# Expert scores: one 512-column pass for the high and low activation parts, the sum of halves on VectorE, the late products on GpSimd

## The reference, cut to what matters

```python
q = (xt @ w_pq).reshape(n_tok, PEER_HEADS, 2, PEER_HALF)
scores = jnp.einsum('thcd,hckd->thck', q, sub_keys)
s_top, i_top = lax.top_k(scores, PEER_TOPK)             # 16 per half
cand = s_top[:, :, 0, :, None] + s_top[:, :, 1, None, :]
best, pos = lax.top_k(cand, PEER_TOPK)                  # 16 experts per token and head
gate = jax.nn.softmax(best, axis=-1)
...
u = jnp.take(expert_u, idx_b, axis=0)
act = jax.nn.gelu(jnp.einsum('thkd,td->thk', u, xb), approximate=False)
v = jnp.take(expert_v, idx_b, axis=0)
return jnp.einsum('thk,thkd->td', g_b * act, v)
```

## Time and profile before

| | |
|---|---|
| Time, median of 3 runs | 2089.2 us (2087.91 to 2093.54) |
| The profiled execution | 2088.83 us, its span 2087.0 us |
| Granted clock of TensorE, mean | 0.993 |
| Busy share | PE 98%, PEld 88%, DVE 71%, ACT 54%, POOL 26% |
| Chain that ended last | PE 82%, POOL 9%, DVE 3%, issue 3% |

### The profile page before, as it was taken

The page is one execution under the profiler, slowest core; times in us unless marked ns, Lnnn a source line. Parts: engine busy times, 40 slices in busy tenths (PEclk is TensorE's granted clock), DMA queues, the critical chain, the costliest instruction groups (busy, mean ns, idle before and its releaser), DMA issues.

```text
span 2087.0 us, 42378 instructions
## 1 busy us (share of the span) xinstructions
PE 2045.3 (98%) x12326; PEld 1829.7 (88%) x12326; DVE 1487.3 (71%) x2388; ACT 1132.3 (54%) x1955; POOL 550.4 (26%) x385
## 2 busy tenths in 40 slices
PE   8999999979999999999999999999999999999997
PEld 6888888767799999999999999987888888888886
DVE  4555766765588879799999999965555555555557
ACT  4455555444455555466666666554555555555553
POOL 0000330010089999944444444100000000000001
PEclk9999999989999999999999999999999999999999
DMA  7755554656576657555555555557756556655554
GB/s 244 228 172 172 171 169 140 225 160 183 160 198 180 184 162 189 167 168 156 157 159 157 157 159 159 167 194 225 213 194 195 193 191 192 194 194 193 192 191 151
DMA packets 254247, 378.47 MB, mean 181 GB/s; under 512 B 41856, under 2 KB 173056, under 8 KB 253568
## 3 DMA queue, kind: packets, MB, share of 16 engines
q1 hardware_dynamic: 254208, 377.98, 60.2%
HBM read 373.69 MB, written 4.19 MB: 181 GB/s over the span
## 4 chain that ended last, share of the span: by engine, by line
PE 82%; POOL 9%; DVE 3%; issue 3%; DMA 1%; SPq 1%; ACT 1%; POOLq 0%; ACTq 0%; DVEq 0%
PE ps L397 26%; PE ps L399 26%; PE ps L398 26%; POOL split_lo L1651 9%; PE ps L626 3%; PE ps L392 1%; DMA raw<-in_expert_v 1%; DMA raw<-in_w_out 0%; DVE split_lo L1012 0%; SPq L370 0%; DVE x_cols L1221 0%; ACT split_hi L701 0%; DVE end_lo L1506 0%; DVE stats L1516 0%; DMA x_nat<-in_x 0%
## 5 line engine op out<-in xcount | busy, mean ns | idle before, releaser
L1012 DVE TENSOR_TENSOR split_lo<-raw,split_hi 128x512 fp32r<-128x512 f32 x848 | 608.5, 720 | 497.0 <-ACT split_hi L701 495.8
L701 ACT ACTIVATE split_hi<-raw 128x512 fp32r<-128x512 f32 x848 | 534.0, 631 | 568.2 <-PE ps L399 552.2
L397 PE MATMUL ps<-act_hi,split_hi 128*128 128x256 f32 x2048 | 586.0, 286 | 0.8 <-POOL split_lo L1651 0.6
L399 PE MATMUL ps<-act_hi,split_lo 128*128 128x256 f32 x2048 | 579.3, 283 | 0.0
L398 PE MATMUL ps<-act_lo,split_hi 128*128 128x256 f32 x2048 | 579.3, 283 | 0.0
L397 PEld LDWEIGHTS ps<-act_hi,split_hi 128*128 128x128 f32 x2048 | 392.6, 192 | 2.6 <-POOL split_lo L1651 1.9
L398 PEld LDWEIGHTS ps<-act_lo,split_hi 128*128 128x128 f32 x2048 | 392.9, 192 | 0.0
L399 PEld LDWEIGHTS ps<-act_hi,split_lo 128*128 128x128 f32 x2048 | 392.6, 192 | 0.0
L397 PE MATMUL ps<-split_hi,whalf_hi 128*128 128x512 f32 x992 | 386.0, 389 | 1.6 <-DVE split_lo L1012 1.6
L398 PE MATMUL ps<-split_lo,whalf_hi 128*128 128x512 f32 x992 | 385.9, 389 | 0.0
L399 PE MATMUL ps<-split_hi,whalf_lo 128*128 128x512 f32 x992 | 385.9, 389 | 0.0
(11 more groups left out here) (183 smaller groups left out, 2101.0 us busy)
## 6 DMA issues: line engine op xcount, KB each, us to landing
raw<-in_expert_u SPq DMA_DIRECT2D x1024, 128.0 KB, 2.9
raw<-in_expert_v SPq DMA_DIRECT2D x256, 512.0 KB, 3.7
raw<-in_w_in SPq DMA_DIRECT2D x112, 512.0 KB, 3.8
raw<-in_w_out SPq DMA_DIRECT2D x32, 512.0 KB, 4.6
raw<-in_w_pq SPq DMA_DIRECT2D x128, 128.0 KB, 2.8
cst<-in_tables SPq DMA_DIRECT2D x3, 768.0 KB, 5.5
x_nat<-in_x SPq DMA_DIRECT2D x4, 512.0 KB, 7.3
x_dram<-x_cols SPq DMA_DIRECT2D x1, 2048.0 KB, 8.0
```

The lines of the kernel that those rows point to most:

```text
L397: nc.tensor.matmul(acc, l_hi, r_hi, start=first, stop=False)
L399: return nc.tensor.matmul(acc, l_lo, r_hi, start=False, stop=last)
L701: nc.scalar.activation(split_hi[:, q % SPLITS, :], raw[:, q // 2, q % 2, :], ACT.Copy).then_inc(hi_ready, 1)
L1012: vec.tensor_tensor(split_lo[:, q % SPLITS, :], raw[:, q // 2, q % 2, :], split_hi[:, q % SPLITS, :].bitcast(f32), ALU.subtract).then_inc( ...
```

## The change

Five things are changed. (1) `act_hi` and `act_lo` lie side by side in `act_both`, and PE does a block with two matmuls: the high part of the weights by 512 columns, which are the 256 of `act_hi` and the 256 of `act_lo`, into the two halves of the bank, and the low part by the 256 columns of `act_hi`, into the first half. (2) DVE adds the halves of the bank with a `tensor_reduce` over two elements that lie 256 apart (`add_halves`) and writes the sum to SBUF; it sends `score_free`. (3) ACT's GELU works in place on that sum. The GELU of a pair's second tile comes after the split of quarter 6 of the next pair, that of the first tile after the split of quarter 2 of the next pair. (4) `late_tile` is POOL's, between `weigh` and `distances`. (5) The first pass of the ranking loop is written out, since pair 0 has no tile before it.

```diff
+            def two(bank, u_hi, u_lo, k):
+                wide = ps[:, bank, :].rearrange("p (a t) -> p a t", a=2)
+                if k < KT - 1:
+                    nc.tensor.matmul(wide, u_hi, act_both[:, :, k, :], start=k == 0, stop=False)
+                    return nc.tensor.matmul(ps[:, bank, 0:SEQ], u_lo, act_hi[:, k, :], start=False, stop=False)
+                nc.tensor.matmul(ps[:, bank, 0:SEQ], u_lo, act_hi[:, k, :], start=False, stop=False)
+                return nc.tensor.matmul(wide, u_hi, act_both[:, :, k, :], start=False, stop=True)
...
             def gelu(pair, t, is_late):
-                act.wait_ge(split_free, pair * 8 + (Q_U + SPLITS + 4 * t + 4))
+                act.wait_ge(score_free, pair * 2 + (t + 3))
                 if is_late:
-                    act.wait_ge(late_used, pair * 2 + (t + 1 - LATE))
-                    dst = late[:, t, :]
+                    dst = late[:, t % 2, :]
...
-                nc.scalar.activation(dst, ps[:, t, 0:SEQ], ACT.Gelu).then_inc(score_free, 1)
+                nc.scalar.activation(dst, dst, ACT.Gelu).then_inc(gelu_done, 1)
...
                 for q in range(4, 8):
                     split_u(pair, q, part_a)
-                gelu(pair, 0, 0 in late_tiles)
+                    if q == 6 and not (isinstance(pair, int) and pair == 0):
+                        gelu(pair, -1, is_late)
...
                 for q in range(1, 4):
                     split_u(pair + 1, q, next_a)
-                gelu(pair, 1, 1 in late_tiles)
+                    if q == 2:
+                        gelu(pair, 0, is_late)
...
+            def add_halves(pair, t, is_late=False):
+                if is_late:
+                    dve.wait_ge(late_used, pair * 2 + (t + 1 - LATE))
+                    dst = late[:, t % 2, :]
+                else:
+                    dst = wexp[:, bass.ds(pair * 2 + t, 1), :].rearrange("p a t -> p (a t)")
+                dve.wait_ge(split_free, pair * 8 + (Q_U + SPLITS + 4 * t + 4))
+                vec.tensor_reduce(dst, ps[:, t % 2, :].rearrange("p (a t) -> p t a", a=2), AX.X, ALU.add).then_inc(score_free, 1)
+
             def split_turn(pair, k, turns=True):
                 split_u(pair, 2 * k)
+                if k == 2:
+                    add_halves(pair, -1, True)
                 split_u(pair, 2 * k + 1)
+                if k == 3:
+                    add_halves(pair, 0, True)
...
                 turn_u(n + 1, 1, True)
+                if not (isinstance(n, int) and n == 0):
+                    add_halves(n, -1)
...
                 turn_u(n + 1, 3, True)
+                add_halves(n, 0)
...
-                        late_tile(pair, -1)
...
-                        late_tile(pair, 0)
...
+                    def late_tile(pair, t, applied):
+                        pool.wait_ge(gelu_done, pair * 2 + (t + 1))
+                        if applied is not None:
+                            pool.wait_ge(gates_free, applied + 2)
+                        row = wexp[:, bass.ds(pair * 2 + t, 1), :].rearrange("p a t -> p (a t)")
+                        eng.tensor_tensor(row, row, late[:, t % 2, :], ALU.mult).then_inc(late_used, 1)
...
                     with pool.Fori(0, GATES // 2 - 1) as i:
                         for s in range(2):
                             weigh(i * 2 + s, s)
+                            late_tile(i + GATE0, s - 1, i * 2 + s)
                             distances(i * 2 + (s + 2), s, True)
```

More of the change, by code:

```diff
@@ L179, in layer_kernel @@
         score_free = sem("score_free")
+        gelu_done = sem("gelu_done")
         x_in = [sem(f"x_in{i}") for i in range(4)]
@@ L600, in score_pair @@
                     for i in range(4):
-                        last = three(ps[:, q // 4, 0:SEQ], split_hi[:, q % SPLITS, i * P:(i + 1) * P],
-                                     split_lo[:, q % SPLITS, i * P:(i + 1) * P], act_hi[:, q % 4 * 4 + i, :],
-                                     act_lo[:, q % 4 * 4 + i, :], q % 4 == 0 and i == 0, q % 4 == 3 and i == 3)
+                        last = two(q // 4, split_hi[:, q % SPLITS, i * P:(i + 1) * P],
+                                   split_lo[:, q % SPLITS, i * P:(i + 1) * P], q % 4 * 4 + i)
                     last.then_inc(split_free, 1)
@@ L897, in keep_set, with u_pair @@
                                      ACT.Copy).then_inc(set_kept, 1)
-            def u_pair(pair, part_a, next_a, late_tiles=(), groups=None, kept=None, staged_set=None):
+            def u_pair(pair, part_a, next_a, is_late=False, groups=None, kept=None, staged_set=None):
                 for q in range(4, 8):
                     split_u(pair, q, part_a)
-                gelu(pair, 0, 0 in late_tiles)
+                    if q == 6 and not (isinstance(pair, int) and pair == 0):
+                        gelu(pair, -1, is_late)
                 if kept is not None:
@@ L918, in _ @@
             act.wait_ge(x1_out, 16)
-            act.sem_inc(late_used, 2)
             act.sem_inc(set_kept, 2)
@@ L945, in _ @@
                 u_pair(i, True, True)
-            u_pair(PAIRS_A - 1, True, False, (1,))
-            u_pair(PICKS, False, False, (0, 1))
+            u_pair(PAIRS_A - 1, True, False)
+            u_pair(PICKS, False, False, True)
             with act.Fori(GATE0 - 1, GATE0 - 1 + GATES // 2) as i:
-                u_pair(i, False, False, (0, 1), i * 2 - (2 * GATE0 - 2))
+                u_pair(i, False, False, True, i * 2 - (2 * GATE0 - 2))
             with act.Fori(GATE0 - 1 + GATES // 2, PAIRS - 1) as i:
-                u_pair(i, False, False, (0, 1))
+                u_pair(i, False, False, True)
             for q in range(4, 8):
                 split_u(PAIRS - 1, q, False)
+                if q == 6:
+                    gelu(PAIRS - 1, -1, True)
             def split_w(n, t, static=False):
@@ L1299, in _ @@
             TOP_STEPS = 30
+            dve.sem_inc(score_free, 2)
+            dve.sem_inc(late_used, 2)
             dve.wait_ge(turn_done, F_Q + 8)
@@ L1339, in rank_set @@
                 turn_u(n + 1, 3, True)
+                add_halves(n, 0)
                 lc.until(second)
                 vec.max_index(head_p[:, s, 8:16], head_b[:, s, 8:16], rest[:, :]).then_inc(ranked, 1)
-            with dve.Fori(0, PH) as i:
+            lc = LoopChain(0, c0, TOP_STEPS)
+            for s in range(2):
+                rank_set(lc, s, s)
+            assert lc.n == TOP_STEPS, lc.n
+            with dve.Fori(1, PH) as i:
                 lc = LoopChain(i, c0, TOP_STEPS)
@@ L1346, in _ @@
                     rank_set(lc, i * 2 + s, s)
-                assert lc.n == TOP_STEPS, lc.n
             chain.n += PH * TOP_STEPS
[L1350 to L1354, removed]
             def apply_gates(n, parity):
@@ L1398, in _ @@
                 turn_u(SOFT + 1, k, True)
+                if k == 1:
+                    add_halves(SOFT, -1)
+            add_halves(SOFT, 0)
             softmax_start()
@@ L1428, in _ @@
                 turn_u(pair, 1, True)
+                add_halves(pair - 1, -1)
                 lc.until(selected[1])
@@ L1432, in _ @@
                 turn_u(pair, 3, True)
+                add_halves(pair - 1, 0)
                 lc.until(collected[1])
@@ L1448, in _ @@
             softmax_end()
+            add_halves(PAIRS_A - 1, -1)
             dve.wait_ge(lo_ready, Q_U + 8 * PAIRS_A)
+            add_halves(PAIRS_A - 1, 0)
             for k in range(2):
@@ L1483, in _ @@
                 split(Q_V, q)
-            late_tile(PAIRS - 1, 0)
+            add_halves(PAIRS - 1, 1, True)
             split(Q_V, 3)
-            late_tile(PAIRS - 1, 1)
             with dve.Fori(0, HELD_AT // 2 - 1) as i:
@@ L1666, in _ @@
                     eng.memset(wexp[:, kept_rows:NT, :], 1.0).then_inc(ones_ready, 1)
+                    pool.wait_ge(ones_ready, 2)
+                    late_tile(PICKS, -1, None)
                     pool.wait_ge(picks_ready, 1)
@@ L1685, in _ @@
                     distances(0, 0, False)
+                    late_tile(PICKS, 0, None)
                     distances(1, 1, False)
+                    late_tile(PICKS + 1, -1, None)
+                    late_tile(PICKS + 1, 0, None)
                     with pool.Fori(0, GATES // 2 - 1) as i:
@@ L1689, in _ @@
                             weigh(i * 2 + s, s)
+                            late_tile(i + GATE0, s - 1, i * 2 + s)
                             distances(i * 2 + (s + 2), s, True)
-                    weigh(GATES - 2, 0)
-                    weigh(GATES - 1, 1)
+                    for s in range(2):
+                        weigh(GATES - 2 + s, s)
+                        late_tile(GATE0 + GATES // 2 - 1, s - 1, GATES - 2 + s)
+                    with pool.Fori(GATE0 + GATES // 2, PAIRS) as i:
+                        for s in range(2):
+                            late_tile(i, s - 1, GATES)
+                    late_tile(PAIRS - 1, 1, GATES)
                 if n == RSTDS:
```

12 lines of the change are left out of this document (2 added, 10 removed).

## The result

The changed kernel takes 2148.08 us (2142.1 to 2150.09), the kernel before beside it 2090.09. The ratio is 1.0269, with a 95% interval of 1.0252 to 1.0286: 2.7% slower. The forecast was 2111, with a range up to 2136. It was slower, as forecast, and the new wait in the gate pairs is there, but two terms of the sum were far off: the gate pairs, and the index loop, which was put at nothing.

The account below looks back on a forecast made before the run. PE was taken to bound ranking and gate pairs, POOL the index loop. Terms -7.7 + 0 - 0.9 + 32 - 1.3 = +22 on the median 2089.2 gave 2111 us, range 2096 to 2136.

Parts of the forecast that it names:

- What bounds the kernel: Score stage: PE sets the ranking and gate pairs (11.52 and 13.29 us), POOL the index loop (11.94 us).
- The change on PE, 0.43 us per pair: Matmul blocks: 0.3467 us instead of 0.360, 0.0133 less, 32 per pair; 27 us over 64 pairs if PE-bound throughout.
- The change on DVE, 0.64 per addition: Each `add_halves` takes 0.64 us (0.6 to 1.2), two per pair; DVE stays under PE or at it.
- The rival of the slow addition: Each addition takes 1.2 us, lengthening ranking, index loop and gate pairs: +76, so 2165 us; chance 0.07.
- The new wait, 14.3 us per gate pair, +32: Gate pairs: PE waits 0.6 us before each gate step; 14.3 instead of 13.29 us per pair, 32 pairs.
- the chain of 7.04 us: Gate step to next: PE, ACT's split, GELU, late product, distances, weigh sum to 7.04 us against PE's own 6.44.
- The step through `add_halves`: Gate step after quarter 1: GELU needs the addition, ready 3.0 us after the step against ACT's 2.97; adds at most 0.1.
- Index loop, 0 (up to +4), and ranking, -7.7: Index loop POOL-bound before and after, so 0, up to +4; ranking and first pairs gain 18 x 0.43 us.
- the two pairs before the gates: The two pairs between index loop and gates: -0.9 us.
- Late products on POOL: Gate pairs: each late product takes 0.74 us on POOL, as work nothing, but POOL runs in order.
- PE as the bound: PE-bound all the way: gate pairs gain 0.43 us like the others, -24, so 2065 us; faster has chance 0.07.
- The third rival: Gate pairs: the chain as said, but each step nearer 7.5 us, 15.0 per pair; +45, so 2134; chance 0.16.

Follow-up runs that it names:

- the wide matmul alone: Kernel before with only the 512-column matmul added; GELU still from the bank's first half, no addition, so the result lacks a product: 2073.37 us, ratio 0.9936.
- distances first: Changed kernel with one swap in GpSimd's gate loop: weigh, distances, late product instead of weigh, late product, distances: 2085.31 us, ratio 0.9987.
- distances first, first pass written out: On top of distances first, the index loop's first pass is written out, with the addition of halves ahead of the compares there: 2082.69 us, ratio 0.9964.
- the kernel with the old pass there: Distances first, but pairs 0 to 25 keep three 256-column matmuls and GELU from PSUM; the additions begin at pair 26: 2076.63 us, ratio 0.9936.

## Why the prediction was wrong, point by point

**What bounds the kernel:** right for the gate pairs and the index loop.

**The change on PE, 0.43 us per pair:** too much. In the kernel with the wide matmul alone it measured 0.25 in the ranking and 0.31 in the gate pairs, since a block costs 0.350 to 0.352, not 0.3467. I had given this as a bound ("if 512 columns behind 256 cost a bit more"). Why the alternation costs 0.004 to 0.005 more stays open.

**The change on DVE, 0.64 per addition:** right. In the changed kernel it lasts 0.652 into `wexp` and 0.677 into `late` (medians), although its two elements lie 1024 bytes apart. The longest of them takes 0.692. The rival of the slow addition is out.

**The new wait, 14.3 us per gate pair, +32:** the mechanism is shown, by taking distances out of the chain (12.96), by shortening one of its two steps (13.94, forecast 13.9) and by lengthening both. The size was 14.85, +48.0. This is the first failed step, 16 us too low: the chain of 7.04 us measured 7.43. By its parts: from the gate products to ScalarE's split 2.59 (1057.75 - 1055.16) instead of 2.47, as TensorE takes 0.92 us from the gate products to the next block behind its wait (1055.16 to 1056.08), not 0.81; GELU 0.41 instead of 0.38; hand-over to GpSimd 0.27 instead of 0.05. The last is the biggest. I had taken it from a hand-over between ScalarE and VectorE with one wait, and it has two waits with register values here, of which the order is worth 0.08. The step through `add_halves` was not the late one.

**Index loop, 0 (up to +4), and ranking, -7.7:** the second failed step, as large. Together with the two pairs before the gates it was -8.6 and measured +7.7. The starts of ScalarE's splits, eight per pair, give the time of each part (us):

| | pairs 0 to 16 | pair 17 | pairs 18 to 25 |
|---|---|---|---|
| before | 193.9 | 11.5 | 95.0 |
| changed | 190.9 | 18.5 | 99.9 |
| distances first | 190.8 | 18.5 | 99.4 |
| distances first, first pass written out | 190.9 | 12.6 | 103.9 |
| changed, first GELU one split earlier | 194.3 | 17.6 | 95.0 |

So the ranking pairs gained about 0.2 each, pair 17 lost 7.0 and the eight pairs of the loop 4.9. The term of the loop was put at 0 because GpSimd sets the pair's time before and VectorE's work with the additions comes to 11.96 us, no more. VectorE's work did not exceed that. Busy time over six passes of its loop, in the kernel before and then in the changed one:

```profile
789.21:857.34 68.13, 67.50 (x551) 66.20 (x550) 62.57 (x62) 34.50 (x60) 67.41 (x46) 1.00 0.78 189
```
```profile
793.09:870.23 77.14, 72.53 (x396) 62.01 (x396) 70.84 (x74) 37.46 (x64) 69.62 (x50) 0.97 0.60 164
```

A pass holds 70.84 / 6 = 11.81 us of VectorE's work but takes 12.86, and no engine is busy all the time any more, GpSimd neither. Before, a pass took 11.36: VectorE ran through the first ones in 10.6 to 11.1, three of them without an idle moment, and only the last ones took the 11.94 of the row I had read. So it came into the loop late and used its slack to catch up. The additions take that slack, while its idle time stays (5.6 us in six passes before, 6.3 after). VectorE's timeline in the kernel before and then in the changed one shows where it comes from:

```profile
856.17 1.25 DVE L1270 STREAM_TRANSPOSE u_cols<-raw 128x1024 f32<-128x1024 f32 x1 [1.26 <-POOL split_lo L1651]
857.34 2.36 DVE L1410 TENSOR_TENSOR onehot<-pos_f,small 128x512 f32<-128x512 f32 x2
```
```profile
855.89 1.25 DVE L1280 STREAM_TRANSPOSE u_cols<-raw 128x1024 f32<-128x1024 f32 x1 [0.89 <-POOL split_lo L1674]
857.06 0.65 DVE L1292 TENSOR_REDUCE wexp<-ps 128x512 f32 x1
857.63 3.19 DVE L1431 TENSOR_TENSOR onehot<-pos_f,small 128x512 f32<-128x512 f32 x2
```

The addition stands behind a transpose that waits for GpSimd. The compares behind it take 3.19 us in this pass instead of 2.36, but over six passes 15.9 instead of 15.1, so their length is the smaller part. The addition returns a bank and releases a GELU, and the waits go round. Waits of the changed kernel between 760 and 910 us (us in total, times, longest):

```profile
ACT wexp L878 <- DVE wexp L1292: 16.0, 7, 6.5
POOL split_lo L1674 <- ACT split_hi L869: 14.5, 13, 5.8
PE ps L598 <- DVE wexp L1292: 11.5, 5, 5.7
DVE u_cols L1280 <- POOL split_lo L1674: 10.5, 13, 1.6
```

ScalarE's GELUs and TensorE wait for the additions, GpSimd for ScalarE, and VectorE for GpSimd. That ring of waits was not in my list. The longest wait is that of pair 17, for the addition behind the softmax's start and the index loop's first operations:

```profile
789.00 0.79 PE L598 MATMUL ps<-act_both,split_hi 128*128 128x512 f32 x1 [5.71 <-DVE wexp L1292]
```

The granted clock from 786 to 797 us is 0.69 behind that wait. That the loss in pairs 0 to 25 comes from the additions and what hangs on them is shown by the kernel with the old pass there (330.2 us) and by the wide matmul without additions (903.9 - 577.3 = 326.7 us to the first gate step). The table's last row shows that the loss of pairs 18 to 25 is not the additions' work as such: every addition is there, only a GELU stands one split earlier, and the pairs take 95.0 us again, while the ranking gets slower by 3.4. Why the GELU's place does both, and which wait of the ring carries the loss, was not tested.

**Late products on POOL:** 0.74 as on the line; the work is hidden, the order isn't. The 0.61 on VectorE in the earlier trace rows holds a stretch of 0.33 us beside GpSimd's `weigh` (1065.38 to 1065.71); where GpSimd has nothing to do, behind the gate steps, the same product takes 0.40 in the kernel before.

**The rivals:** PE as the bound was met in the gate pairs with distances first, and nowhere in the index loop with the additions. The third rival, steps nearer 7.5, described the gate stage best, and even its total (2134) left out the index loop. The range should have added a bad index loop to a bad chain.

## What to carry to other kernels

When work goes to an engine that has time, look at what is queued behind its wait: here one line's place in a loop was worth 58 us of gate stage, while the work itself cost nothing. Reckon a loop over several engines with measured hand-overs into that very engine, and take the sum of an engine's work as a lower bound. In the index loop that sum was right and the pass still took 1 us more, since VectorE's waits for GpSimd stayed and what was put behind them held up other engines. And where a buffer's return moves from one engine to another, go through the new engine's whole order for the longest stretch in front of it.

## What the hardware showed that was not expected

- A matmul of 512 columns and one of 256 in turn cost 0.350 to 0.352 us together (wide matmul alone), against 0.3467 from rows of each kind.
- With a wait of TensorE of 0.7 us in every 7.4 (changed kernel) the granted clock of the gate stage was 1.00; with one of 2.03 us in every 10.4 (both GELUs one split later) it was 0.85, with blocks 0.64 us apart and a granted clock of 0.50 behind the wait.
- The late product, two inputs of 256 elements, took 0.40 us on VectorE with GpSimd idle (kernel before, behind the gate steps). Beside GpSimd's distances (late products on VectorE) it took 1.70 when it started 0.47 us behind them, and 0.40 when it started with them, but then they took 2.19 instead of 1.90. The candidates' sum took 0.38 or 1.11, by its place. The additions took 0.64 to 0.69 throughout the changed kernel.
